# A scan whose engines follow one common order, and the same scan with an order for each engine

## What is computed

```python
def step(state, inp):
    r_t, d_t, k_t, v_t, kk_t, a_t = inp
    sa = jnp.einsum('bhvk,bhk->bhv', state, -kk_t)
    state = (state * d_t[:, :, None, :] + sa[..., None] * (kk_t * a_t)[:, :, None, :]
             + v_t[..., None] * k_t[:, :, None, :])
    return state, jnp.einsum('bhvk,bhk->bhv', state, r_t)
...
y = ((y - mean) * lax.rsqrt(var + GN_EPS)).reshape(B, S, D) * ln_g + ln_b
bonus = jnp.sum(rf * kf * r_k, axis=-1, keepdims=True) * vf
out = (y + bonus.reshape(B, S, D)) * g.astype(jnp.float32)
return out.astype(h.dtype) @ w_o
```

## Time and profile before

| | us |
|---|---|
| median of 3 runs | 954.66 |
| lowest, highest | 953.49, 959.54 |
| the profiled execution | 954.78 |
| its span | 953.0 |
| mean granted clock | 0.945 |

### The profile page before, as it was taken

One profiled execution on the slowest core, in us unless ns is written; L12 is line 12 of the kernel. 1 busy time (PEld: TensorE's weight loads), 2 busy tenths in 40 slices (PEclk: granted clock), 3 DMA queues, 4 the chain that ended last, 5 costly groups with the idle time before them and its releaser, 6 DMA issues.

```text
span 953.0 us, 18108 instructions
## 1 busy us (share of the span) xinstructions
PE 833.8 (87%) x7723; PEld 726.1 (76%) x7723; DVE 666.9 (70%) x735; ACT 421.0 (44%) x597; POOL 118.8 (12%) x180
## 2 busy tenths in 40 slices
PE   1599999666878998999999989997778899999997
PEld 0597898665767777999999879884546599999975
DVE  4897885756556658999999675676774667655452
ACT  3269333333434454444444465424662734444441
POOL 8500013423132040000000022200000000000000
PEclk9799999887879999999999999997989999999999
DMA  8932236231221256999999258752000568555641
GB/s 323 328 117 89 90 134 210 85 106 53 83 91 47 68 181 230 368 384 366 373 369 357 98 193 252 218 200 91 1 1 2 176 218 282 199 186 178 194 158 44
DMA packets 71839, 170.20 MB, mean 179 GB/s; under 512 B 5432, under 2 KB 6736, under 8 KB 71760
## 3 DMA queue, kind: packets, MB, share of 16 engines
q1 hardware_dynamic: 68784, 160.75, 48.6%
q0 software_dynamic: 2416, 7.15, 2.6%
q10 hardware_dynamic: 560, 1.14, 0.3%
HBM read 166.42 MB, written 1.05 MB: 176 GB/s over the span
## 4 chain that ended last, share of the span: by engine, by line
PE 57%; DVE 28%; ACT 8%; issue 3%; DMA 2%; POOL 0%; ACTq 0%; DVEq 0%; POOLq 0%
DVE wlo L1072 7%; PE ps L1634 6%; PE ps L1623 6%; PE ps L1636 6%; PE ps L1638 6%; PE ps L1626 6%; PE ps L1625 6%; DVE acc L1315 2%; DVE acc L1011 2%; ACT whi L663 2%; PE ps L1564 2%; PE ps L1566 2%; PE ps L1567 2%; DVE gt L1011 1%; DVE prob L1422 1%
## 5 line engine op out<-in xcount | busy, mean ns | idle before, releaser
L1072 DVE TENSOR_TENSOR wlo<-raw,whi 128x2048 fp32r<-128x2048 f32 (+1 forms) x98 | 216.1, 2205 | 54.5 <-ACT whi L663 52.3
L663 ACT ACTIVATE whi<-raw 128x2048 fp32r<-128x2048 f32 (+1 forms) x98 | 179.9, 1842 | 129.7 <-DMA raw<-in_mlp_down_dram 88.1
L1623 PE MATMUL ps<-ghi,whi 128*128 128x256 f32 x576 | 163.3, 284 | 3.9 <-DVE wlo L1072 1.7
L1626 PE MATMUL ps<-ghi,wlo 128*128 128x256 f32 x576 | 163.0, 283 | 0.0
L1625 PE MATMUL ps<-glo,whi 128*128 128x256 f32 x576 | 163.0, 283 | 0.0
L1623 PEld LDWEIGHTS ps<-ghi,whi 128*128 128x128 f32 x576 | 110.5, 192 | 7.1 <-issue 5.0
L1625 PEld LDWEIGHTS ps<-glo,whi 128*128 128x128 f32 x576 | 110.5, 192 | 0.5
L1626 PEld LDWEIGHTS ps<-ghi,wlo 128*128 128x128 f32 x576 | 110.5, 192 | 0.0
L1634 PE MATMUL ps<-whi,hidhi 128*128 128x512 f32 x256 | 101.5, 396 | 2.4 <-DVE wlo L1072 2.4
L1636 PE MATMUL ps<-whi,hidlo 128*128 128x512 f32 x256 | 100.5, 393 | 0.0
L1638 PE MATMUL ps<-wlo,hidhi 128*128 128x512 f32 x256 | 100.2, 392 | 0.0
(11 more groups left out here) (351 smaller groups left out, 1618.5 us busy)
## 6 DMA issues: line engine op xcount, KB each, us to landing
raw<-in_mlp_up_dram SPq DMA_DIRECT2D x32, 1024.0 KB, 5.7
raw<-in_mlp_down_dram SPq DMA_DIRECT2D x32, 1024.0 KB, 5.2
raw<-in_ada_w_dram SPq DMA_DIRECT2D x24, 1024.0 KB, 5.7
late<-in_ada_w_dram SPq DMA_DIRECT2D x24, 1024.0 KB, 9.3
late<-in_kv_ada_w_dram SPq DMA_DIRECT2D x8, 1024.0 KB, 8.4
raw<-in_kv_w_dram SPq DMA_DIRECT2D x6, 1024.0 KB, 5.3
raw<-in_rw_k_dram SPq DMA_DIRECT2D x4, 1024.0 KB, 9.8
raw<-in_rw_r_dram SPq DMA_DIRECT2D x4, 1024.0 KB, 5.0
```

Source lines behind the costliest of these rows:

```text
L663: ins = sc.activation(whi[i][:, ks, :], raw[i][:, :].rearrange("p (k n) -> p k n", k=4)[:, ks, :], ACT.Copy)
L1072: ins = dv.tensor_tensor(wlo[i][:, ks, :], raw[i][:, :].rearrange("p (k n) -> p k n", k=4)[:, ks, :], whi[i][:, ks, :].bitcast(F32), ALU.s ...
L1623: mm(out_, whi[b][:, k, cols], hi[:, k0 + k, :], start=(first and k == 0 and m % 2 == 0), stop=False, skip_group_check=True)
L1626: ins = mm(out_, wlo[b][:, k, cols], hi[:, k0 + k, :], start=False, stop=False, skip_group_check=True)
```

## The change

`scan_schedule()` and its list are gone. Each step is a function on each engine (`z_step(c, h, level)` and so on), and each engine calls its own in an order of its own, written out. The orders differ from engine to engine; of the two levels of a chunk's halves one may now run ahead of the other. With that:

- `copy` and `values` on ACT, `mask` and `bonus` on DVE are split into two calls each. `copy` and `values` count their semaphores twice as often. ACT's copy of chunk 2 now stands behind the first two z of chunk 1.
- POOL gets waits of its own for `begin_step` and `level_step`.
- PE's turn step waits for the blocks copied to `xtr` as well. ACT's first `piece_high` waits for PE's s step of the last but one chunk too.
- The out-projection's block 0 goes to banks 4 and 5 and its gate row to banks 0 and 1; `post_norm` takes the bank by `Y_BANK`. Its wait for the last zs falls away. The place of the eight `project` steps on PE is nearly the same, all behind u of the last chunk; the gate row is now before the last of them.

The core of the diff, ACT's copy step before and after, one line of ACT's order, and the projection:

```diff
-        SCAN = scan_schedule()
+        Y_BANK = lambda b, k: 2 * b if b or k > 1 else 4
...
-                if what == "copy":
-                    act.wait_ge(s_kr, c + 1)
-                    if c >= 2:
-                        act.wait_ge(s_y_ps, c - 1)
-                    for e in range(2):
-                        rows = slice(64 * e, 64 * e + 64)
-                        ins = sc.activation(knr[par][rows, :, e, :, :].rearrange("p j a t -> p j (a t)"),
-                                            krF[rows, c, :, :, :].rearrange("p j a t -> p j (a t)"), ACT.Copy)
-                    ins.then_inc(s_krc, 1)
...
+            def copy_step(c, h):
+
+                par = c % 2
+                act.wait_ge(s_kr, c + 1)
+                if c >= 2:
+                    act.wait_ge(s_y_ps, c - 1)
+                rows = slice(64 * h, 64 * h + 64)
+                sc.activation(knr[par][rows, :, h, :, :].rearrange("p j a t -> p j (a t)"),
+                              krF[rows, c, :, :, :].rearrange("p j a t -> p j (a t)"), ACT.Copy).then_inc(s_krc, 1)
...
+                if c == 0 and h == 0:
+                    act.wait_ge(s_y_ps, NCH - 1)
+                    act.wait_ge(s_st_ps, NCH - 1)
+                weight_high(12 + c, h)
...
+            z_step(1, 1, 0); z_step(1, 0, 1); copy_step(2, 0); copy_step(2, 1); centre_step(0); z_step(1, 1, 1)
...
-                    ins = token_block(12 + n, 0, slice(0, 512), ps[:, ch, :], zhi, zlo, 4 * kh, kh == 0,
-                                      range(2 * part, 2 * part + 2))
...
+                ins = token_block(12 + n, 0, slice(0, 512), ps[:, 4 + ch, :], zhi, zlo, 4 * kh, kh == 0,
+                                  range(2 * part, 2 * part + 2))
```

More of the change, by code:

```diff
@@ new lines, in s_step, with y_step @@
+            def s_step(c):
+                par = c % 2
+                act.wait_ge(s_st, c + 1)
+                for e in range(2):
+                    rows = slice(64 * e, 64 * e + 64)
+                    ins = sc.activation(sv[1 - par][rows, :, e, :], state[rows, :, :], ACT.Copy)
+                ins.then_inc(s_state_sv, 1)
+            def y_step(c):
+                act.wait_ge(s_y_ps, c + 1)
+                sc.activation(yF[:, :, N * c:N * c + N], bank(7).rearrange("p (j t) -> p j t", j=KC),
+                              ACT.Copy).then_inc(s_y, 1)
@@ L1261, in post_norm @@
                     cols = slice(512 * half, 512 * half + 512)
[L1262 removed]
+                    st.do(dv.tensor_tensor(pn[:, cols], ps[:, Y_BANK(b, k) + half, :], gate[:, cols], ALU.mult))
                 row_rnorm(b)
@@ new lines, in z_step @@
+            def z_step(c, h, level):
+                par = c % 2
+                js = range(4 * h, 4 * h + 4)
+                mine = [(j, e) for j in js for e in range(2)]
+                pe.wait_ge(s_xc[h], 5 * c + level + 1)
+                if level:
+                    pe.wait_ge(s_tt[h], 5 * c + level)
+                else:
+                    pe.wait_ge(s_ts[h], c + 1)
+                for j, e in mine:
+                    rows, across, n = slice(64 * e, 64 * e + 64), slice(64 - 64 * e, 128 - 64 * e), j - 4 * h
+                    ins = mm(ps[across, 2 * h, N * n:N * n + N], xc[(level + 1) % 2][rows, j, :], tt[par][rows, h, 1, n, :],
+                             start=True, stop=True)
+                ins.then_inc(s_z_ps[h], 1)
@@ new lines, in u_step @@
+            def u_step(c):
+                par = c % 2
+                pe.wait_ge(s_w, c + 1)
+                for i in range(2):
+                    pe.wait_ge(s_tt[i], 5 * c + 5)
+                if c:
+                    pe.wait_ge(n_z, c)
+                else:
+                    pe.wait_ge(n_bv, 1)
+                for j, e in heads:
+                    rows = slice(64 * e, 64 * e + 64)
+                    across = slice(64 - 64 * e, 128 - 64 * e)
+                    ins = mm(ps[across, 7, N * j:N * j + N], tt[par][rows, j // 4, 0, j % 4, :], wc[rows, j, :],
+                             start=True, stop=True)
+                ins.then_inc(s_u_ps, 1)
```

651 lines of the change are left out of this document (346 added, 305 removed).

## The result

The changed kernel takes 910.16 us (median of four executions, 906.71 to 911.35); the kernel before 954.08 beside it. The ratio is 0.9545, with a 95% interval of 0.9514 to 0.9576: 43.9 us less. I had forecast 916, from 903 to 936. The profiled execution is the fastest of the four (906.71 us, span 905.0, mean granted clock 0.967), so its span is 48.0 us shorter than before.

What follows compares the result with a forecast made beforehand. No engine full in the 160.2 us scan; order and waits set its length, DVE second bound. Work 101.6 + idle 15 + lower clock 5.1 = 121.7 us, 38.5 less: 954.8 - 38.5 = 916 us, range 903 to 936.

Steps and rivals of the forecast that it cites:

- The bound and the split: Scan, 160.2 us: 101.6 PE work at full clock, 19.0 excess of the lower clock, 39.6 PE idle; no engine full.
- Everything behind moves up whole: Behind the scan: all later work is released by its tail and moves earlier by the scan's full saving, 38.5 us.
- The copy: ACT, chunk 1: copies to knr at 11.5 to 13.6 us after the start step, no longer waiting for PE's y.
- The walk: Scan orders stepped at full clock: 7.6 us idle, scan 109.2; as rival near 904 us, chance 0.2.
- The idle term of 15 us: PE idle in the scan: 7.6 us walked, plus the 3.1 us "issue" wait and about 1 us per chunk for handoffs.
- The clock term of 5.1 us: Scan: lower-clock excess falls from 19.0 to 5.1 us, keeping two stretches of 6.8 us at 0.37 us per us.
- the rule that I weighed: PE clock in the scan: frequent short waits could keep the excess at 19 us, 14 us above the sum.
- The work at full clock: PE in the scan: no matmul or vector operation is added, so 101.6 us of work stay.
- The banks, and piece 15: Out-projection: new banks bring no time; weight piece 15, loaded after DVE's ada(11), lands about 14 us after last tt, hidden.
- the signs: Changed trace: scan 115 to 130 us, u to u 29 to 33, PE idle about 15, granted clock above 0.92.
- no gain: Rival: the scan's waits move to other places in the same sum, 950 to 960 us; chance 0.05.
- half of it: Rival: PE and DVE hold each other up; idle 25, lower clock 12, scan 138.6, total 933 us; chance 0.2.

Runs made afterwards that it cites:

- The late copy alone: Kernel before with ACT's copies to knr for chunks 2 and 3 moved three slots later, behind y: 942.91 us, ratio 0.9910.
- the one with the masks early: Kernel before with ACT's copies to knr late and DVE's masks of the next chunk one place earlier: median 947.59 us, ratio 0.9955.
- copy and ada version: Kernel before with ACT's copies to knr late and DVE's ada pieces of chunks 1 and 2 behind tt: 944.57 us, ratio 0.9939.
- the changed kernel again: The changed kernel itself, unedited, measured again on the chip of the follow-up runs: 908.50 us, ratio 0.9562.

## Why the prediction was right, step by step

**The bound and the split.** That the whole gain had to come from the scan's idle time and its clock held: scan -46.9 of -48.0 us, projections 25.86 for 25.77, behind u(3) 631.1 for 632.2. "Everything behind moves up whole" held to about a microsecond.

**The copy.** I had placed y's end 9.8 us behind the start step of chunk 1, the copies at 11.5 to 13.6, with no wait. The start step is at 183.39; y's copy begins 9.7 us behind it, the copies run from 11.2 to 13.3. The late copy alone, on the old list, is worth 8.5 us: the largest single piece found, and a fifth of the gain.

**The walk.** From the first start to that of chunk 1: 22.5 us walked, 22.8 measured. u to u: 28.1 walked, 28.7 measured in chunk 1; 29.1 and 31.7 in chunk 2; 2.5 and 1.3 us idle in chunk 3. Chunk 2's excess of 2.6 us is in two rows: the stall of 1.93 us and 1.7 us from the stretch at the lower clock behind it. Idle 7.6 walked; 6.3, 8.2 and 8.6 in the three profiles with the new orders. This agreement is in good part luck. The walk has no "issue" stalls, and of the measured idle time they are 3.9, 5.2 and 5.9 us. What is left to order and handoffs is 2.4 to 3.0 us, some 5 less than walked: up to the start step of chunk 1 it is 1.7 us in after where I had 4.3, in chunk 3 1.3 where I had 2.5.

**The idle term of 15 us was mis-sized.** It was the walk with 7.4 us of allowances: 3.1 for the stall "issue", and a microsecond per chunk for handoffs, because "DVE and PE are both full, so a late tt is not caught up". The stall is there (3.7 us in three places of L1798, 1.9 at most). The allowance for handoffs was not needed, and the walk's own 7.6 us were too many: DVE is busy 95.3 of 113.3 us and has slack, by the run with 6 us more on it. I had compared DVE's 28.1 us per chunk with PE's 28, but of the seven ada operations of chunk 1 four are left, and it has 23.7 us there now. That the ada pieces come later stood in the change's own rows; the sum didn't use it.

**The clock term of 5.1 us** measured 3.4, and 1.7 in two further profiles. Its reason, half of the idle goes and so does the low clock, was too simple: the profiles with the ada pieces or the masks moved have less idle time than the late copy alone and more of the lower clock, though both are of longer executions than is typical for their version. As to the rule that I weighed: the Trainium skill, TensorE: Matmul & The Clock Gate, "A second HAM failure mode: psum-queue depth-cycling", has frequent short idle times make the clock change back and forth. The profiles of the intermediate versions fit it (37.6, 47.9 and 54.7 us at the lower clock, in several stretches, with waits of up to 2.5 and 4.4 us for tt), but no run separates short waits from long ones. In the changed kernel the waits are few, PE is busy for 94% of the scan, and the 14 us that the rule would have added are not there.

**The work at full clock** came out at 103.6 to 104.8 us where I had 101.6 kept. Nothing was added; the matmuls' ends are modelled, so that 2 to 3 us of very short gaps can count as work here and as idle there. I can't tell these apart. Over all versions without added work this term comes to 100.9 to 104.8 us while the excess goes from 1.4 to 25.0, so counting half of the busy time at the lower level as excess holds to a few microseconds.

**The banks, and piece 15**: nothing, as said, and hidden, as said: PE is busy 25.63 of the 25.86 us of the projections.

**The rivals.** By its terms the result lies nearer the walk than my sum: scan 113 to 115 us, where the walk gives 109.2 and I had 121.7. 910 is halfway between 916 and 904. Two of the signs lie outside what I had written: the scan at 113.3 us where I had 115 to 130 (114.4 and 115.1 in the two further profiles), and two of the three chunks, 28.7 and 25.7 us (the third 31.7) where I had 29 to 33. Both come from the idle term. The rival "no gain" counts 10.5 us of idle time with three causes in chunk 1; the rows' 4.7, 2.8 and 2.7 make 10.2, which changes nothing in it. That PE and DVE hold each other up ("half of it") asked for 25 us of idle and 12 of excess; they are 6.3 and 3.4.

**What stays open.** Of the single moves tried on the old list, the best brings 8.5 us of 44, and the two put on top of it brought nothing more. The other 35 came with all orders together; which smallest set of moves brings them, no run here shows. That more of the lower clock stands where the gain of a single move should be is in the rows of two such versions, of one profile each, both longer than their median. In the one with the masks early the late tt is in it too. Why the low stretches came just there is open.

## What to carry to other kernels

Before a re-order, split the busiest engine's time in a latency-bound stage into work at full clock, excess of the lower clock and idle time, and walk the new order with the rows' own durations: here the walk's total was closer than the walk with cautious allowances, but check it term by term: stalls that it didn't have made up for waits that it had too long. When a single move takes a wait away and the time doesn't fall, look at what the other waits and the granted clock did before giving the idea up, and see first whether the profiled execution is a typical one of its version: three of the readings above rest on longer ones. And charge an engine by what the new order gives it in each chunk, not by what it had there.

## What the runs showed of the hardware

**Less waiting, lower clock.** In its profile the copy and ada version has 4.7 us less idle time on PE than the late copy alone, and 10.3 us more at the lower level. In its two long stretches at 0.50 PE is busy for 95% of the time, in the changed kernel's for 100% (3.40 of 3.40 us at 237.00), so a full PE didn't bring the clock back at once. In the changed kernel both falls come behind a wait: of 1.96 us that ended at 160.60, with the fall at 161.90, and of 1.93 us that ended at 235.45, with the fall at 237.00. A wait of that length doesn't always bring one: in the second profile of the changed kernel one of 2.00 us ended at 172.28, and its only stretch at the lower level is the one from 161.5 to 165.0.

**Stalls without a releaser.** They sit in the middle of a run of small matmuls of one step. In the timelines of PE, first of before (chunk 1), then of after (chunks 1 and 2), then of the changed kernel again:

```profile
212.07 0.28 PE L1774 MATMUL ps<-knr,sv 128*64 128x64 f32 x3 [3.07 <-issue]
```

```profile
197.09 0.27 PE L1798 MATMUL ps<-tt,zs 64*64 64x64 f32 x1 [1.18 <-issue]
...
235.45 0.27 PE L1798 MATMUL ps<-tt,zs 64*64 64x64 f32 x1 [1.93 <-issue]
```

```profile
199.36 0.27 PE L1798 MATMUL ps<-tt,zs 64*64 64x64 f32 x1 [1.32 <-issue]
...
237.72 0.27 PE L1798 MATMUL ps<-tt,zs 64*64 64x64 f32 x1 [1.66 <-issue]
```

With the new orders these two stand at the same place of PE's program each time, behind its matmuls number 1007 and 2010 of the scan, in after, in the changed kernel again and with the banks put back (0.77 and 0.84 us there). The place is fixed and the length is not.

One queue of instructions moves 16 KB packets, 24 of them in the scan of before and 24 in that of after, 160.2 and 113.3 us long with the same 3,007 matmuls: the packets follow PE's work and not the time. Between the two stalls of after lie 1003 matmuls and eight of these packets. One moves shortly ahead of each of the two (at 194.8 and 232.95, the stalls begin at 195.91 and 233.52); in before one moves 0.8 us behind the begin of the stall (209.8 for 209.0). But most packets have no stall beside them, and with the old orders in the changed kernel's code the stall of 3.1 us is not there (chunk 1 has 42.65 us for 45.95). That the stalls are PE waiting for its own instructions is what the fixed place suggests; no run here settles it.

**POOL.** Its level blocks take 726 ns in chunk 1 of the new order and 921 in that of the old, for the same shape. Why was not looked into: PE waits for POOL only ahead of start steps, 1.6 us in the scan of before and 2.0 in after.
